# Hybrid encoder trunk on one core: the FFN up projection of two column groups by seven block products in place of eight

## What is computed

```python
h = rmsnorm(x, pre_ffn_g[l])
f = (jax.nn.silu(h @ w_ffn_gate[l]) * (h @ w_ffn_up[l])) @ w_ffn_down[l]
x = x + rmsnorm(f, post_ffn_g[l])
```

## Time and profile before

| | |
|---|---|
| median of 3 runs | 818.06 us (817.89 to 818.13) |
| the profiled execution's own time | 818.09 us |
| its span in the trace | 816.3 us |
| PE busy | 805.7 us, 99% of the span |
| DVE busy | 538.1 us, 66% |
| ACT busy | 428.3 us, 52% |
| DMA | 148.09 MB, mean 181 GB/s |

### The profile page before, as it was taken

How to read it: one execution, slowest core, us unless ns; L and a number is a source line. 1 busy time by engine, 2 the same in 40 slices (tenths; PEclk the granted TensorE clock), 3 DMA queues, 4 the chain that set the end, 5 groups by cost and what they waited for, 6 DMA issues and landing times.

```text
span 816.3 us, 10484 instructions
## 1 busy us (share of the span) xinstructions
PE 805.7 (99%) x4298; PEld 677.1 (83%) x4298; DVE 538.1 (66%) x549; ACT 428.3 (52%) x559; POOL 66.1 (8%) x127
## 2 busy tenths in 40 slices
PE   8999999999999999999999999999999999999997
PEld 5897898888888888888879889988888888888885
DVE  5799898556666464645488869975568645645652
ACT  6467968634454343443445788875326434343431
POOL 2841000000220000000011100000003000000000
PEclk9999999999999999999999999999999999999999
DMA  9876454444449465653476735444554556555511
GB/s 290 255 245 205 147 176 158 155 155 155 141 168 309 155 221 196 203 169 141 155 224 213 260 128 182 155 159 155 186 172 155 189 198 227 186 191 182 194 52 51
DMA packets 80049, 148.09 MB, mean 181 GB/s; under 512 B 7185, under 2 KB 27777, under 8 KB 80002
## 3 DMA queue, kind: packets, MB, share of 16 engines
q1 hardware_dynamic: 80000, 147.42, 54.4%
q10 hardware_dynamic: 2, 0.00, 0.0%
HBM read 146.36 MB, written 1.05 MB: 181 GB/s over the span
## 4 chain that ended last, share of the span: by engine, by line
PE 91%; DVE 3%; POOL 3%; issue 1%; ACT 0%; DMA 0%; DVEq 0%; POOLq 0%; ACTq 0%
PE work L646 17%; PE work L647 17%; PE work L648 17%; PE acc L646 8%; PE acc L648 8%; PE acc L647 8%; PE work L638 3%; PE work L639 3%; PE work L640 3%; POOL turned_by L531 1%; PE work L786 1%; PE acc L711 1%; PE work L734 1%; PE acc L724 1%; DVE weights_lo L1324 1%
## 5 line engine op out<-in xcount | busy, mean ns | idle before, releaser
L1324 DVE TENSOR_TENSOR weights_lo<-weights_raw,weights_hi 128x2048 fp32r<-128x2048 f32 x132 | 302.1, 2293 | 155.5 <-ACT weights_hi L959 155.4
L959 ACT ACTIVATE weights_hi<-weights_raw 128x2048 fp32r<-128x2048 f32 x132 | 252.6, 1916 | 197.7 <-PE work L648 115.0
L646 PE MATMUL work<-weights_hi,act_a_hi 128*128 128x512 f32 x544 | 214.3, 394 | 0.0
L648 PE MATMUL work<-weights_hi,act_a_lo 128*128 128x512 f32 x544 | 212.0, 390 | 0.0
L647 PE MATMUL work<-weights_lo,act_a_hi 128*128 128x512 f32 x544 | 211.9, 390 | 0.0
L646 PEld LDWEIGHTS work<-weights_hi,act_a_hi 128*128 128x128 f32 x544 | 102.2, 188 | 21.9 <-issue 1.0
L648 PEld LDWEIGHTS work<-weights_hi,act_a_lo 128*128 128x128 f32 x544 | 102.1, 188 | 21.4
L647 PEld LDWEIGHTS work<-weights_lo,act_a_hi 128*128 128x128 f32 x544 | 102.2, 188 | 20.4
L646 PE MATMUL acc<-weights_hi,act_b_hi 128*128 128x512 f32 x240 | 94.2, 393 | 0.0
L648 PE MATMUL acc<-weights_hi,act_b_lo 128*128 128x512 f32 x240 | 93.5, 390 | 0.0
L647 PE MATMUL acc<-weights_lo,act_b_hi 128*128 128x512 f32 x240 | 93.4, 389 | 0.0
(11 more groups left out here) (178 smaller groups left out, 885.1 us busy)
## 6 DMA issues: line engine op xcount, KB each, us to landing
weights_raw<-in_w_in SPq DMA_DIRECT2D x43, 1024.0 KB, 5.2
weights_raw<-in_w_ffn_down SPq DMA_DIRECT2D x22, 1024.0 KB, 4.9
weights_raw<-in_w_ffn_gate SPq DMA_DIRECT2D x20, 1024.0 KB, 5.1
weights_raw<-in_w_ffn_up SPq DMA_DIRECT2D x20, 1024.0 KB, 5.2
weights_raw<-in_w_pa SPq DMA_DIRECT2D x8, 1024.0 KB, 5.0
weights_raw<-in_w_pb SPq DMA_DIRECT2D x8, 1024.0 KB, 5.0
weights_raw<-in_w_o SPq DMA_DIRECT2D x8, 1024.0 KB, 4.8
weights_raw<-in_w_ffn_gate SPq DMA_DIRECT2D x4, 512.0 KB, 4.0
```

The source lines that it names most:

```text
L646: mm(dst, xh, wh, start=first, stop=False)
L648: return mm(dst, xl, wh, start=False, stop=final)
L959: activate(w_hi[:, SLOT[n], :], raw[:, n % RAW, :], ACT.Copy).then_inc(hi_done.sem, 1)
L1324: v.tensor_tensor(w_lo[:, SLOT[n], :], raw[:, n % RAW, :], bits(w_hi[:, SLOT[n], :]), ALU.subtract).then_inc(split_done.sem, 1)
```

## The change

Groups 1 and 2, and groups 3 and 4, form two units u = 0, 1 in each layer. The up product of a unit is a 2 x 2 block product: two token tiles by two row halves, times two row halves by two column groups. It was eight block products (two for each of four fu panels); it is now seven, `("s", 7u)` to `("s", 7u + 6)`, each of 12 matmuls of 512 columns on 128 tokens (`s_product`, L820 of the new kernel).

- Four of the seven take sums of blocks of x. DVE makes them once a layer (`x_sums`: the whole of hi + lo, 128 x 2048, then four differences of 128 x 512), ACT rounds them (`x_sums_hi`), DVE takes the rest (`x_sums_lo`).
- Four take sums of weight blocks. DVE makes two per unit in the raw slot (`block_sum`, 128 x 2048, after the splits of s0 and s2); the other two are made by accumulating transfers of 1 MB, issued from POOL's queue (`add_block`), which read the block from DRAM again and add it to the raw slot. ACT's split of s5 and s6 waits for them.
- Three partial sums per unit are copied from PSUM by ACT (`unit_copy`) and combined on DVE (`unit_add`) ahead of `f_product`.
- Two arrays of other stages (`q_feat`, `lru_a`) serve as raw slots 3 and 4 in the FFN. The banks are now written out with each use: fg pairs of groups 1 to 4 lie in banks 2 and 3. The panels' order, and with it every engine's walk, is new from fg2 on; ring slots are skipped at pa0, pb0 and fgu0 in place of fg4. The gain load for the last norm comes earlier on SP's queue.
- At the start of layer 1, ACT splits panel q0's first half ahead of the last norm, DVE splits it by halves, and PE waits half by half.

In the fences below: the core of the diff.

```diff
-    for c in range(groups):
-        plan += [("fg", 2 * c), ("fg", 2 * c + 1), ("fu", 2 * c), ("fu", 2 * c + 1)]
-        if c:
-            plan += [("down", 2 * c - 2), ("down", 2 * c - 1)]
-    plan.remove(("down", 2 * groups - 3))
-    plan += [("fgu", 0), ("fgu", 1)]
+    plan += [("fg", 0), ("fg", 1), ("fu", 0), ("fu", 1)]
+    plan += [("fg", 2), ("fg", 3), ("s", 0), ("s", 1), ("down", 0), ("s", 2), ("fg", 4), ("s", 3), ("fg", 5)]
+    plan += [("s", 4), ("s", 5), ("down", 1), ("s", 6)]
+    plan += [("fg", 6), ("fg", 7), ("s", 7), ("s", 8), ("down", 2), ("s", 9), ("down", 3), ("fg", 8), ("s", 10)]
+    plan += [("fg", 9), ("s", 11), ("down", 4), ("s", 12), ("down", 5), ("s", 13)]
+    plan += [("fgu", 0), ("fgu", 1), ("down", 6)]
     plan += [("down", j) for j in range(2 * groups - 3, 2 * groups + 1)]
     return plan
...
+def block_loads(plan):
+    loads = []
+    for name, j in plan:
+        if name != "s":
+            loads.append((name, j))
+        elif j % 7 == 0:
+            u = 4 * (j // 7)
+            loads += [("b", u), ("b", u + 2)]
+        elif j % 7 == 1:
+            loads.append(("b", 4 * (j // 7) + 1))
+        elif j % 7 == 2:
+            loads.append(("b", 4 * (j // 7) + 3))
+    return loads
...
-    for c in range(1, groups):
-        uses += [(name, 2 * d + t) for name, d in (("fg", c), ("fu", c), ("turn_f", c - 1)) for t in range(2)]
-    n = 2 * groups
-    return uses + [("fgu", 0), ("fgu", 1), ("turn_f", n - 2), ("turn_f", n - 1), ("turn_f", n)]
+    uses = [(use, k % 4) for k, use in enumerate(uses)]
+    def two(name, n, b):
+        return [((name, n), b), ((name, n + 1), b + 1)]
+    uses += two("fg", 2, 2) + two("turn_f", 0, 0) + [(("sa", 0), 0), (("sb", 0), 1), (("sd", 0), 1)] + two("fg", 4, 2)
+    uses += two("fg", 6, 2) + two("turn_f", 2, 0) + [(("sa", 1), 0), (("sb", 1), 1)] + two("turn_f", 4, 2)
+    uses += [(("sd", 1), 1)] + two("fg", 8, 2)
+    uses += two("fgu", 0, 2) + two("turn_f", 6, 0) + two("turn_f", 8, 0) + [(("turn_f", 10), 2)]
+    return uses
...
+        def raw_slot(s):
+            if s < RAW:
+                return raw[:, s, :]
+            return (QT, AG)[s - RAW][:, :, :].rearrange("p k s -> p (k s)")
...
-        skips = [AT["fg", 2 * c] for c in range(2, 2 + -NPAN % RING)]
+        skips = [AT["pa", 0], AT["pb", 0], AT["fgu", 0]][:-NPAN % RING]
...
+                    slot, last_read = PRIOR[n]
+                    if last_read is not None:
+                        sp.wait_ge(*split_done.at(l, last_read + 1))
+                    elif slot == RAW:
+                        sp.wait_ge(*x_done.at(l, 2))
+                    else:
+                        sp.wait_ge(*xs_summed.at(l, 4))
...
+                def add_block(u, i, to, what):
+                    c = 512 * (2 * u + 1 + what // 2)
+                    src = w_ffn_up[l][512 * (what % 2):512 * (what % 2) + 512, c:c + 512]
+                    nc.gpsimd.dma_start(raw_slot(RAW_OF["b", 4 * u + to]).rearrange("p (k f) -> p k f", k=4),
+                                        src.rearrange("(k p) f -> p k f", p=P), accum_op=ALU.add
+                                        ).then_inc(sum_loaded[i].sem, 16)
...
+                    if m == 4:
+                        for u in range(2):
+                            pool.wait_ge(*summed.at(l, 2 * u + 1))
+                            add_block(u, 5, 2, 3)
+                            pool.wait_ge(*split_done.at(l, AT["s", 7 * u + 3] + 1))
+                            add_block(u, 6, 0, 1)
...
+                            if xa is not None and i == 0:
+                                pe.wait_ge(*xa_done.at(l, xa + 2 * t + (j - j0) + 1))
+                            ks = range(4)
+                            if t == 0 and name in halved:
+                                pe.wait_ge(*head_split.at(l, j - j0 + 1))
+                                t_panel_product(name, j, dst, hi, lo, t, range(2))
+                                ks = range(2, 4)
...
+                def s_product(u, i):
+                    n = AT["s", 7 * u + i]
+                    wh, wl = t_panel(w_hi, SLOT[n], 4), t_panel(w_lo, SLOT[n], 4)
+                    if i == 0:
+                        dst = claim(l, "sa", u)
+                    elif i == 1:
+                        dst = claim(l, "sb", u)
+                    elif i == 2:
+                        dst = claim(l, "sd", u)
+                    elif i == 3:
+                        dst = bank("sa", u)
+                        pe.wait_ge(*s_copied.at(l, 3 * u + 1))
+                    elif i == 4:
+                        dst = bank("sd", u)
+                        pe.wait_ge(*s_copied.at(l, 3 * u + 2))
+                    elif i == 5:
+                        dst = bank("sa", u)
+                        pe.wait_ge(*s_copied.at(l, 3 * u + 3))
+                    else:
+                        dst = bank("sa", u)
+                        pe.wait_ge(*s_added.at(l, 3 * u + 3))
+                    if i == 2:
+                        pe.wait_ge(*xs_split.at(l, 4))
+                    split_ready(n)
+                    for k in range(4):
+                        if i in (0, 1, 6):
+                            ks, cols = k + (0 if i == 0 else 4), slice(P if i == 6 else 0, 2 * P if i == 6 else P)
+                            xh, xl = xn_hi[:, ks, cols], xn_lo[:, ks, cols]
+                        else:
+                            which = {2: 0, 3: 2, 4: 3, 5: 1}[i]
+                            xh, xl = xs_hi[:, which, k, :], xs_lo[:, which, k, :]
+                        adds = i >= 3
+                        mm(dst[:, :], xh, wh[:, k, :], start=k == 0 and not adds, stop=False, skip_group_check=adds)
+                        mm(dst[:, :], xh, wl[:, k, :], start=False, stop=False, skip_group_check=adds)
+                        last = mm(dst[:, :], xl, wh[:, k, :], start=False, stop=k == 3, skip_group_check=adds)
+                    last.then_inc(panel_used.sem, 1)
...
+                for n in range(AT["fg", 2], AT["down", 2 * GROUPS - 3]):
+                    name, j = PLAN[n]
+                    if name in ("fg", "fgu"):
+                        if j % 2 == 0:
+                            gate_banks = [claim(l, name, j + t)[:, :] for t in range(NT)]
+                        elif name == "fg" and (j // 2) % 2 == 1:
+                            turn_f(j // 4)
+                        elif name == "fgu":
+                            turn_f(GROUPS - 2)
+                        t_product(name, j, gate_banks, xn_hi, xn_lo)
+                        if (name, j) == ("fgu", 1):
+                            turn_f(GROUPS - 1)
+                    elif name == "s":
+                        s_product(j // 7, j % 7)
+                        if j == 8:
+                            turn_f(2)
...
+                def x_sums_hi():
+                    for i in range(4):
+                        act.wait_ge(*xs_summed.at(l, i + 1))
+                        done(activate(xs_hi[:, i, :, :], (s_first, s_third, s_second, s_fourth)[i], ACT.Copy),
+                             xs_hi_done, i + 1)
...
+                def unit_copy(u, i):
+                    name, step_, dst = {0: ("sa", 1, p1_t), 2: ("sd", 2, p5_t), 3: ("sa", 3, u2_t)}[i]
+                    act.wait_ge(*panel_used.at(l, AT["s", 7 * u + i] + 1))
+                    if u:
+                        act.wait_ge(*f_up.at(l, PRODUCT[2 * u, 1] if i == 2 else PRODUCT[2 * u - (i == 0), 0]))
+                    elif i == 2:
+                        act.wait_ge(*xs_split.at(l, 4))
+                    done(activate(dst, bank(name, u)[:, :], ACT.Copy), s_copied, 3 * u + step_)
...
+                if name == "s" and j % 7 in (0, 2):
+                    block_sum(l, j // 7, j % 7)
+            def block_sum(l, u, i):
+                to, what = {0: (0, 2), 2: (0, 3)}[i]
+                dve.wait_ge(*raw_loaded[RAW_OF["b", 4 * u + what]].at(l, LOADED_AT["b", 4 * u + what]))
+                into = raw_slot(RAW_OF["b", 4 * u + to])
+                v.tensor_tensor(into, into, raw_slot(RAW_OF["b", 4 * u + what]), ALU.add).then_inc(summed.sem, 1)
...
+                def unit_add(u, odd, t):
+                    if odd:
+                        dve.wait_ge(*panel_used.at(l, AT["s", 7 * u + 1] + 1))
+                        dve.wait_ge(*s_copied.at(l, 3 * u + 1))
+                        done(v.tensor_tensor(p1_t, bank("sb", u)[:, :], p1_t, ALU.add), s_added, 3 * u + 1)
+                        dve.wait_ge(*s_added.at(l, 3 * u + 1))
+                        return p1_t
+                    name, part, i, m = ("sd", u2_t, 4, 2) if t == 0 else ("sa", p5_t, 5, 3)
+                    dve.wait_ge(*panel_used.at(l, AT["s", 7 * u + i] + 1))
+                    dve.wait_ge(*s_copied.at(l, 3 * u + 3))
+                    done(v.scalar_tensor_tensor(part, bank(name, u)[:, :], -1.0, part, ALU.mult, ALU.subtract),
+                         s_added, 3 * u + m)
```

(46 more changed lines are left out.)

196 lines of the change are left out of this document (133 added, 63 removed).

## The result

| | before | after |
|---|---|---|
| median | 817.97 us (817.18 to 818.13, 4 runs) | 834.43 us (833.78 to 835.52, 4 runs) |
| ratio | | 1.0205, interval 1.0187 to 1.0222: slower, by about 2% |
| profiled execution, its span | 818.09, 816.3 us | 834.85, 833.1 us |

A forecast was written before the change was run, and what follows sets the result against it. PE was taken as the bound all through. From 818.1 us: -10.9 matmuls, -0.7 layer 1's start, +23.2 waits ahead of fg2, +4.0 low clock, 0 for other DVE work and transfers, giving 833.7 us; range 829 to 840.

The forecast's parts named there:

- Fewer matmuls: Up products of four units: 84 in place of 96 matmuls each, at 0.227 us, all on PE's path: -10.9 us.
- Start of layer 1: PE's late second matmul at layer 1's start comes in time through q0's earlier split by halves: -0.7 us (0 to -1).
- The wait ahead of fg2: PE waits in each layer for DVE's second f_product, behind ten added operations: 11.6 us each, +23.2 us.
- The clock: After each wait ahead of fg2, four us at half speed lose 2.0: +4.0 us; bounds nothing or 3.9 each.
- The rest of DVE's work: From fg2 to s6, 42 us of DVE work (81%) fit beside PE's 51.7 us: 0.
- The accumulating transfers: POOL's 1 MB adds to raw blocks, tightest for s6: 14.8 us allowed, bounds 5.2 and 20, taken as hidden: 0.
- PE does not wait: Rival: no wait ahead of fg2 as the second f_product is done by 247.8; only the saving remains, 806.5 us; chance 0.06.

The follow-up runs named there:

- e7: The kernel before with both the exchanged banks from fg2 on and ten added DVE operations on arrays nobody reads, still eight products: 845.66 us, 1.0346.
- e5: The kernel before with only banks 0, 1 and 2, 3 exchanged in every use from fg2 on: 824.09 us, 1.0082.
- e1: The changed kernel with banks 0, 1 and 2, 3 exchanged in every use from fg2 on, DVE's order untouched: 823.00 us, 1.0063.
- e2: The changed kernel with DVE's second f_product of group 0 straight behind its silu, banks as changed: 817.68 us, 0.9995.
- e4: The changed kernel with 95 transposes of the identity into a free bank ahead of fg2, results unused: 830.79 us, 1.0157.
- e3: The changed kernel with both edits, banks exchanged from fg2 on and the second f_product early: 821.31 us, 1.0042.
- e8: e3 with the split of the turned input ahead of the split of down0, and the x sums' remainders behind that: 816.51 us, 0.9981.
- e9: e8 with the first addition and product of unit 0 moved ahead of the splits and block sum it stood behind on DVE: 810.02 us, 0.9902.
- e11: e9 with the second accumulating transfer of the first unit issued twice in each layer: 834.10 us, 1.0197.
- e12: e9 with the bank swap taken back, DVE's order kept: 815.44 us, 0.9968.
- e6: The kernel before with only ten added DVE operations of the new sums' sizes at their places, on arrays nobody reads: 819.96 us, 1.0026.

## Why the prediction was right

The forecast was 15.6 us over before; the profiled executions differ by 16.8.

- *Fewer matmuls*, -10.9: 48 fewer at the same pitch; e7 less the change, 11.2, agrees within what else differs between the two.
- *Start of layer 1*, -0.7: measured -1.0, since a second step, of 0.58, shrank with the first.
- *The wait ahead of fg2*, 2 x 11.6: measured 2 x 11.5. The sum of starts over DVE's list gave 17.5 for 17.4. e5 to e7 show that it takes the bank and the list together, e1 and e2 what is left when one is taken away.
- *The clock*, +4.0: measured 1.7 and 2.7; e4 gave 3.6 back. The 2.0 each came from another place, the kernel's start, and long pauses in these runs cost from 1.4 to 2.9, so that the two add up to nearly 4.0 is in part luck. The Trainium skill (TensorE: Matmul & The Clock Gate, the section on HAM oscillation) has a price for each gap that sends the gate to its lower level. The trace agrees: its two gaps cost 1.7 and 2.7 us, and in e2 the pauses of 2.5 us cost 1.6 and 1.7.
- *The rest of DVE's work*, 0: right for the time and wrong in its reason. I had laid 42 us of work against 51.7 us of PE's and concluded that it fits. It fits only because the wait of 11.5 us let DVE get ahead, which the prediction names beside a rival but leaves out of its sum. With the wait gone the same work was late three times over, at the turned input (e3), at the first addition (e8) and at a gate panel (e9). An order of work, not an amount, was the limit: e9 has every operation of e3 and takes 11.3 us less.
- *The accumulating transfers*, 0: right, with its reason. The tightest one landed after 9.8 us (9.1 in layer 1), inside the bounds of 5.2 and 20 and under the 14.8 allowed. The two halves of that 14.8 were 24.5 us from issue to s6, measured 24.6, and 9.7 for the chain behind the landing, measured 8.5 in e11 (ACT and DVE overlap in it). That leaves 16.1 us in the change, and 14.0 in e9, where s6 comes 22.5 us after the issue. e11 shows that the limit is real.
- *Left out of the sum*: an earlier start (-0.5), the slower matmuls on sums of x (+1.1) and 0.7 spread thin. They cancel in part.
- Of the rivals, PE does not wait, 806.5, is what e9 nearly reaches.

## What to carry to other kernels

When work is added to an engine that runs in order, find for each operation that releases something (a bank, a buffer) what now stands ahead of it, and add up starts to starts: here that gave the wait within 0.1 us. When a wait is then taken away, make the same list again for each release behind it. The wait had been hiding them, and a busy share of 72% says nothing about them. An algorithm that saves 1.3% of the time in matmuls was worth +2.0% or -1.0% by nothing but the places of a few operations in one queue and a pair of banks.

## What the runs showed of the hardware that I had not expected

A matmul is not quite the same price for each source. In the changed kernel, one line in two forms (ns of one: least, median, most):

```profile
L854 PE MATMUL work<-weights_hi,x_sums x64: 390/394/404, 283.2 to 777.8; 128*128 128x512 f32 x64
L854 PE MATMUL work<-weights_hi,act_a_hi x48: 389/389/389, 272.3 to 786.0; 128*128 128x512 f32 x48
```

And twelve of one product in order of time, the first and the last:

```profile
283.16 0.40 PE L854 MATMUL work<-weights_hi,x_sums 128*128 128x512 f32 x1
...
285.72 0.40 PE L856 MATMUL work<-weights_hi,x_sums 128*128 128x512 f32 x1
```

Eleven steps take 2.56 us, 0.233 each, where others take 0.227. Over 192 such matmuls that is 1.1 us. Whether it is where the array lies, its layout or the shorter run per block was not tried.

A pause of 2.5 us can bring the lower level, 1.2 GHz, and need not: it did in both layers in e2's profile and in e12's, in one of two in e5's, and by the mean clocks of e12's twelve runs in 14 of 24 cases (that reads each run's mean clock as two falls, one or none). The same kernel took 813.0 to 817.0 us with it. Steps of 1.2 us (e4 and e6) did not in either profile. And an accumulating transfer of 1 MB that followed another to the same buffer landed after 13.9 us in both layers, where one alone took 8.6 to 10.7 (all of them in the change, e9 and e11); whether the buffer or what ran beside it is the reason was not tried.
